# A mixer layer's projections: high and low parts of the activations side by side in one matmul, the two halves summed on VectorE

## The reference

```python
x = x + 0.5 * gate * swiglu(mod(norm(x)), ffn1)        # y (context) the same
hc = mod(norm(y));  pc = hc @ w_in[:, :3072]           # keys fwd, keys bwd, values
s_f, s_b = final states of the two gated recurrences over the context
hx = mod(norm(x));  px = hx @ w_in                     # 8192 columns
o  = bidirectional gated recurrence (8 heads) from px[:, :4096], starting at s_f, s_b
mix = concat(norm(o) * silu(px[:, 4096:5120]), hyena(px[:, 5120:]))
x = x + gate * (mix @ w_out)
x = x + 0.5 * gate * swiglu(mod(norm(x)), ffn2);  return norm(x)
```

## Time and profile before

| | |
|---|---|
| median of 3 runs | 2997.64 us (2997.46 to 2998.92) |
| span of the profiled execution, first to last instruction | 2996.3 us |
| time of the profiled execution beside its span | not recorded |
| TensorE busy | 2959.0 us, 15850 matmuls |
| VectorE busy | 2027.5 us |
| ScalarE busy | 1159.4 us |
| context, HGRN and Hyena stages | 1556.0 to 2152.2 us |

### The profile page before, as it was taken

The page is one execution under the profiler, slowest core; times in us unless marked ns, Lnnn a source line. Parts: engine busy times, 40 slices in busy tenths (PEclk is TensorE's granted clock), DMA queues, the critical chain, the costliest instruction groups (busy, mean ns, idle before and its releaser), DMA issues. The chain is left out here.

```text
span 2996.3 us, 42446 instructions
## 1 busy us (share of the span) xinstructions
PE 2959.0 (99%) x15850; PEld 2521.0 (84%) x15850; DVE 2027.5 (68%) x2558; ACT 1159.4 (39%) x1473; POOL 148.3 (5%) x182
## 2 busy tenths in 40 slices
PE   7999999999999999999999999999999999999998
PEld 3588888888888888888889999999997888888887
DVE  4698667676766677774476567778866666666667
ACT  5322222222122222222247777754445444444444
POOL 3000000000000000000000033340000000000000
PEclk9999999999999999999999999999999999999999
DMA  9865546354566758573335554455565666666664
GB/s 368 333 210 185 180 140 198 128 175 147 161 222 220 253 167 278 187 242 98 97 90 175 174 168 149 150 161 179 166 204 166 187 194 189 189 190 189 192 192 155
DMA packets 369832, 558.00 MB, mean 186 GB/s; under 512 B 17764, under 2 KB 259809, under 8 KB 368946
## 3 DMA queue, kind: packets, MB, share of 16 engines
q1 hardware_dynamic: 364256, 543.05, 57.7%
q0 software_dynamic: 2640, 8.52, 0.9%
q10 hardware_dynamic: 2818, 4.82, 0.4%
HBM read 550.02 MB, written 6.30 MB: 186 GB/s over the span
## 5 line engine op out<-in xcount | busy, mean ns | idle before, releaser
L442 DVE TENSOR_TENSOR w_lo<-raw,w_hi 128x1024 fp32r<-128x1024 f32 x736 | 911.8, 1240 | 696.1 <-ACT w_hi L435 693.9
L435 ACT ACTIVATE w_hi<-raw 128x1024 fp32r<-128x1024 f32 x736 | 777.9, 1059 | 1478.3 <-PE bank L454 1095.0
L711 DVE SCALAR_TENSOR_TENSOR states<-ada_raw,silu_c,states 128x1024 f32<-128x1024 f32 x300 | 375.5, 1281 | 2.3
L452 PE MATMUL bank<-h_hi_early,w_hi 128*128 128x512 f32 x768 | 300.7, 392 | 2.1 <-issue 2.1
L454 PE MATMUL bank<-h_hi_early,w_lo 128*128 128x512 f32 x768 | 298.9, 389 | 0.0
L453 PE MATMUL bank<-h_lo_early,w_hi 128*128 128x512 f32 x768 | 298.8, 389 | 0.0
L458 PE MATMUL bank<-w_hi,h 128*128 128x512 f32 x736 | 287.7, 391 | 1.9 <-DVE h L559 1.3
L460 PE MATMUL bank<-w_lo,h 128*128 128x512 f32 x736 | 286.5, 389 | 0.0
L459 PE MATMUL bank<-w_hi,h 128*128 128x512 f32 x736 | 286.3, 389 | 0.0
L452 PE MATMUL bank<-h_hi_late,w_hi 128*128 128x512 f32 x704 | 274.0, 389 | 0.0
L454 PE MATMUL bank<-h_hi_late,w_lo 128*128 128x512 f32 x704 | 273.9, 389 | 0.0
(11 more groups left out here) (345 smaller groups left out, 4978.7 us busy)
## 6 DMA issues: line engine op xcount, KB each, us to landing
raw<-in_ffn_w_dram SPq DMA_DIRECT2D x528, 512.0 KB, 4.3
ada_raw<-in_ada_w_dram SPq DMA_DIRECT2D x252, 512.0 KB, 4.7
raw<-in_w_in_dram SPq DMA_DIRECT2D x176, 512.0 KB, 3.7
raw<-in_w_out_dram SPq DMA_DIRECT2D x32, 512.0 KB, 4.3
ada_ahead<-in_ada_w_dram SPq DMA_DIRECT2D x20, 512.0 KB, 17.6
raw<-in_ada_w_dram SPq DMA_DIRECT2D x8, 512.0 KB, 18.4
ada_more<-in_ada_w_dram SPq DMA_DIRECT2D x8, 512.0 KB, 6.9
spec<-spec_spill POOLq DMA_DIRECT2D x8, 512.0 KB, 3.9
```

Source lines behind the costliest of these rows:

```text
L435: nc.scalar.activation(w_hi[un.slot(j)][:], raw[un.slot(j)][:], ACT.Copy).then_inc(hi_done, 1)
L442: nc.vector.tensor_tensor(w_lo[un.slot(j)][:], raw[un.slot(j)][:], w_hi[un.slot(j)][:].bitcast(F32), ALU.subtract).then_inc(lo_done, 1)
L452: nc.tensor.matmul(o, w_hi[slot][:, c0:c0 + P], hi, start=start, stop=False, skip_group_check=True)
L711: nc.vector.scalar_tensor_tensor(out=total, in0=src, scalar=silu_c[:, m, t:t + 1], in1=total, op0=ALU.mult, op1=ALU.add).then_inc(done, 1)
```

## The change

The activations' parts become two halves of one tensor (`hc`, `hx`), and so do the weights' (`w_parts`). For a weight block, `paired_unit` has one matmul of 512 moving columns (both halves of the activations times `w_hi`, into a whole bank) and one of 256 (`w_lo` times the high part, onto the first half of the bank). `value_unit` has one of 512 (`w_hi` and `w_lo` side by side move) and one of 256. A part then fills two banks, and parts take banks 0, 1 and 2, 3 in turn. The two halves of a result are summed by VectorE: `join` reduces two banks (1024 numbers a partition) to 512 in SBUF, `join_values` does the same in two instructions, straight to `ctok` or `vtok` in place of ScalarE's copy. ScalarE and the edges read the sum. Joins stand ahead of `rest_unit` in VectorE's step after the part's last unit; the gates, `xq` and `xg` move from j = 3, 7, 11, 19 to j = 4, 8, 12, 20, the context's from 3 (7 for the first pair) and 7 to 4 and 8. TensorE waits for a join before it starts the part after the next. `w_out` and the FFNs keep their matmuls.

```diff
-        w_hi = [sb(f"w_hi{s}", [P, UNIT], F32R) for s in range(RING)]
-        w_lo = [sb(f"w_lo{s}", [P, UNIT], F32R) for s in range(RING)]
+        w_parts = sb("w_parts", [P, 2, RING, UNIT], F32R)
+        w_hi = [w_parts[:, 0, s, :] for s in range(RING)]
+        w_lo = [w_parts[:, 1, s, :] for s in range(RING)]
...
-        hc_hi = sb("hc_hi", [P, KB, CTX], F32R, scope=con)
-        hc_lo = sb("hc_lo", [P, KB, CTX], F32R, scope=con)
+        hc = sb("hc", [P, 2, KB, CTX], F32R, scope=con)
+        hc_hi, hc_lo = hc[:, 0], hc[:, 1]
...
+        x_whole = sb("x_whole", [P, 2, SEQ], scope=hgs)
...
 
-        def value_unit(pe, un, j, kg, o, hi, lo, each=None):
+        def value_unit(pe, un, j, kg, base, hi, lo):
+
+            pe.wait_ge(lo_done, un.number(j) + 1)
+            for k in range(4):
+                kb = 4 * kg + k
+                w0 = k * 256
+                for t in range(TB):
+                    own = slice(t * P, (t + 1) * P)
+                    nc.tensor.matmul(bank[base + t], hi(kb)[:, own], w_parts[:, :, un.slot(j), w0:w0 + 256], start=(kb == 0), stop=False,
+                                     skip_group_check=True)
+                    last = nc.tensor.matmul(bank[base + t][:, 0:256], lo(kb)[:, own], w_hi[un.slot(j)][:, w0:w0 + 256], start=False,
+                                            stop=(kb == KB - 1), skip_group_check=True)
+            last.then_inc(w_used, 1)
+
+        def paired_unit(pe, un, j, kg, base, both, hi, each=None):
 
             pe.wait_ge(lo_done, un.number(j) + 1)
             for k in range(4):
                 kb = 4 * kg + k
                 if each:
                     pe.wait_ge(each, kb + 1)
-                w0 = k * 256
-                for t in range(TB):
-                    own = slice(t * P, (t + 1) * P)
-                    out_t = o[:, t * 256:(t + 1) * 256]
-                    nc.tensor.matmul(out_t, hi(kb)[:, own], w_hi[un.slot(j)][:, w0:w0 + 256], start=(kb == 0 and t == 0), stop=False,
+                for b in range(2):
+                    c0 = k * 256 + b * P
+                    nc.tensor.matmul(bank[base + b], w_hi[un.slot(j)][:, c0:c0 + P], both(kb), start=(kb == 0), stop=False,
                                      skip_group_check=True)
-                    nc.tensor.matmul(out_t, lo(kb)[:, own], w_hi[un.slot(j)][:, w0:w0 + 256], start=False, stop=False,
-                                     skip_group_check=True)
-                    last = nc.tensor.matmul(out_t, hi(kb)[:, own], w_lo[un.slot(j)][:, w0:w0 + 256], start=False, stop=(kb == KB - 1),
-                                            skip_group_check=True)
+                    last = nc.tensor.matmul(bank[base + b][:, 0:256], w_lo[un.slot(j)][:, c0:c0 + P], hi(kb), start=False,
+                                            stop=(kb == KB - 1), skip_group_check=True)
             last.then_inc(w_used, 1)
 
-        def by_head(bank_ap):
-
-            return bank_ap.rearrange("p (a h c) -> p h a c", a=TB, h=2)
+        def join(out, base):
+
+            return nc.vector.reduce_sum(out, banks[:, base:base + 2, :].rearrange("p a (s n) -> p a n s", s=2), mybir.AxisListType.X)
+
+        def join_values(out, base):
+
+            for a in range(TB):
+                ins = nc.vector.reduce_sum(out[:, :, a, :], bank[base + a].rearrange("p (s h c) -> p h c s", s=2, h=2), mybir.AxisListType.X)
+            return ins
 
         def last_sq(kb):
...
+        OUT_BANK = 4
+        CTX_TURN = (4, 7)
+        HG_JOINED, HY_JOINED = 2 * PAIRS, 7 * PAIRS
         MEAN_BANK = (7,) * (PAIRS - 1) + (6,)
...
+        def hg_base(it, part):
+            return 2 * ((5 * it + part) % 2)
+
+        def hy_base(p, c):
+            return 2 * ((3 * p + c) % 2)
 
         def out_unit(k):
...
+                n = 5 * it + j // 4
+                if j % 4 == 0 and n == 0:
+                    pe.wait_ge(joined, 2 * PAIRS)
+                elif j % 4 == 0 and n == 1:
+                    pe.wait_ge(cs["v"], 1 + PAIRS)
+                elif j % 4 == 0:
+                    pe.wait_ge(joined, HG_JOINED + n - 1)
                 if j // 4 == 3:
-                    value_unit(pe, MX, 20 * it + j, j % 4, bank[3][:], lambda k: hx_hi[:, k, :], lambda k: hx_lo[:, k, :])
+                    value_unit(pe, MX, 20 * it + j, j % 4, hg_base(it, 3), lambda k: hx_hi[:, k, :], lambda k: hx_lo[:, k, :])
                 else:
-                    col_unit(pe, MX, 20 * it + j, j % 4, [bank[j // 4][:, 0:256], bank[j // 4][:, 256:512]],
-                             lambda k: hx_hi[:, k, :], lambda k: hx_lo[:, k, :], True)
+                    paired_unit(pe, MX, 20 * it + j, j % 4, hg_base(it, j // 4), lambda k: hx[:, :, k, :], lambda k: hx_hi[:, k, :])
 
             def hg_scores(it, sc):
...
-            def gates(s, d, b, k_ap, g_ap, value):
-
-                ac.wait_ge(w_used, value)
-                nc.scalar.activation(k_ap, bank[b][:], ACT.Sigmoid, scale=-1.0)
-                nc.scalar.activation(g_ap, bank[b][:], ACT.Sigmoid).then_inc(s["gate"], 1)
+            def gates(s, whole, count, k_ap, g_ap):
+
+                ac.wait_ge(joined, count)
+                nc.scalar.activation(k_ap, whole, ACT.Sigmoid, scale=-1.0)
+                nc.scalar.activation(g_ap, whole, ACT.Sigmoid).then_inc(s["gate"], 1)
...
@@ -1919,7 +1956,7 @@
                     for d in range(2):
                         if j == gates_at[d]:
                             ac.wait_ge(cs["kd"], 2 * it)
-                            gates(cs, d, d, flat(ck[:, d]), flat(cg[:, d]), used(un, CTX_END[it][d]))
+                            gates(cs, flat(c_whole[d][:]), 2 * it + d + 1, flat(ck[:, d]), flat(cg[:, d]))
...
 
-                if j in (3, 7):
-                    d = j // 4
-                    gates(xs, d, d, flat(xk[it % 2][:, d]), flat(xa[it % 2][:, d]), used(MX, 20 * it + j))
                 if j in (4, 8):
                     d = j // 4 - 1
+                    gates(xs, flat(x_whole[:]), HG_JOINED + 5 * it + d + 1, flat(xk[it % 2][:, d]), flat(xa[it % 2][:, d]))
                     keys_logs(xs, it, d, flat(xk[it % 2][:, d]), flat(xa[it % 2][:, d]), hg_cols[:, it])
-                if j == 11:
+                if j == 12:
                     if it:
                         ac.wait_ge(xs["kq"], it * 10)
-                    ac.wait_ge(w_used, used(MX, 20 * it + j))
-                    nc.scalar.activation(flat(xq[:]), bank[2][:], ACT.Copy, scale=DK ** -0.5).then_inc(xs["v"], 1)
-                if j == 15:
-                    ac.wait_ge(w_used, used(MX, 20 * it + j))
-                    if it:
-                        ac.wait_ge(xs["ope"], it)
-                    nc.scalar.activation(vtok[:].rearrange("p (h a) c -> p h a c", h=2), by_head(bank[3][:]), ACT.Copy
-                                         ).then_inc(xs["v"], 1)
-                if j == 19:
+                    ac.wait_ge(joined, HG_JOINED + 5 * it + 3)
+                    nc.scalar.activation(flat(xq[:]), flat(x_whole[:]), ACT.Copy, scale=DK ** -0.5).then_inc(xs["v"], 1)
+                if j == 20:
                     if it:
                         ac.wait_ge(xs["mix"], it + 1)
-                    ac.wait_ge(w_used, used(MX, 20 * it + j))
-                    nc.scalar.activation(flat(xg[:]), bank[4][:], ACT.Silu).then_inc(xs["v"], 1)
+                    ac.wait_ge(joined, HG_JOINED + 5 * it + 5)
+                    nc.scalar.activation(flat(xg[:]), flat(x_whole[:]), ACT.Silu).then_inc(xs["v"], 1)
                 if j + 3 in KEY_AT[it][1:]:
                     hg_decays(it, KEY_AT[it].index(j + 3) - 1)
                 if j == READ_AT[it] + 1:
...
                 if j in CONV_AT[p]:
                     c = CONV_AT[p].index(j)
-                    ac.wait_ge(w_used, used(MX, T_HY + 12 * p + 4 * c + 3))
+                    n = 3 * p + c
+                    ac.wait_ge(joined, HY_JOINED + n + 1)
...
-                        ins = nc.scalar.activation(conv[p % 2][:, c, b, :], bank[part_bank(p, c)][:, b * 256:(b + 1) * 256], ACT.Identity,
+                        ins = nc.scalar.activation(conv[p % 2][:, c, b, :], u_whole[n % 2][:, b, :], ACT.Identity,
...
 
+            def ctx_joined(it, d):
+
+                ve.wait_ge(w_used, used(Units(U_CTX, it, 12), CTX_END[it][d]))
+                if it:
+                    ve.wait_ge(cs["gate"], 2 * it + d - 1)
+                join(c_whole[d][:], ctx_base(it, d)).then_inc(joined, 1)
+
+            def ctx_values(it):
+
+                ve.wait_ge(w_used, used(Units(U_CTX, it, 12), 11))
+                if it:
+                    ve.wait_ge(cs["st"], it)
+                join_values(ctok[:, 2].rearrange("p (h a) c -> p h a c", h=2), ctx_base(it, 2)).then_inc(cs["v"], 1)
+
             for it in range(PAIRS):
                 un = Units(U_CTX, it, 12)
                 ve.wait_ge(cs["k"], 2 * it)
```

(37 more changed lines are left out.)

97 lines of the change are left out of this document (50 added, 47 removed).

## The result

The changed kernel takes 3020.39 us (median of 4 runs, 3018.86 to 3022.87) against 2997.66 us before: ratio 1.0076, 95% interval 1.0064 to 1.0088. It is slower, by 22.7 us; the forecast was 14 us slower.

A forecast was written before the change was run, and what follows sets the result against it. TensorE was taken as the bound while VectorE and ScalarE keep ahead. 2996.3 us less 18.4 saved plus 32.5 of stalls gave a 3010.4 us span, a median of 3011.7, say 3012 us; forecast's own range 3004 to 3025, wider range 2985 to 3026.

The forecast's parts named there:

- What bounds the kernel: Whole span: TensorE busy 2959.0 of 2996.3 us; less matmul time shortens the run if ScalarE and VectorE stay ahead.
- The sum: Whole span: 2996.3 less 18.4 saved plus 32.5 us of stalls gives 3010.4, as a median 3011.7 us.
- The saving: Projection matmuls: a weight block takes 346.9 instead of 360.0 ns; 1408 blocks give 18.4 us less.
- The cost of a join: VectorE: 1.24 us per two-bank join, 51 us more work in all, on average hidden in its free time.
- The delay: ScalarE's inputs wait behind VectorE's queued joins: 7.9 us of stalls per whole HGRN period, 32.5 us in all.
- The distance is enough: Rival: the other engines stay far enough ahead; 2979 us, or 2990 with stalls at the tightest places alone; chance 0.22.
- Half the stalls: Rival: fewer table loads or less `xg` delay leave stalls of 13 to 25 us; 2992 to 3004 us; chance 0.17.
- The clock falls: Rival: stalls lower TensorE's clock, up to 13.6 us more, 2 to 4 expected; above 3025 us; chance 0.08.
- The pace doesn't change: Rival: matmul pairs run at three times 120.0 ns, so nothing is gained; 3021 us; chance 0.05.

The follow-up runs named there:

- The run with idle joins: Changed kernel with HGRN joins omitted, ScalarE reading only first halves from PSUM, and same-size VectorE reductions that nobody reads in the joins' places; 3002.39 us, ratio 1.0014.
- Three places: Changed kernel with query join before `w_lo` of t = 31, `xg` at t = 41, part 0's gates and logarithms at t = 45 and 46; 3003.85 us.
- all places: Changed kernel with query join, `xg`, both parts' HGRN gates and logarithms, and joins around the Hyena stage moved; values still joined; 2994.30 us, ratio 0.9987.
- the values apart and the context stage's logarithms moved: All-places kernel with HGRN values as three unjoined 256-column matmuls and the first context pair's logarithms at step 9 instead of 8; 2989.07 us, ratio 0.9971.
- the waits filled: Changed kernel with 512-column matmuls into an unused bank before waits where TensorE idled from t = 39 on; 3019.73 us, ratio 1.0071.

## Why the prediction was right, and where its numbers were off

**What bounds the kernel** was right: time taken from TensorE counts only as long as the other two keep their distance, and they did not.

**The sum.** The span was forecast at 3010.4 us and is 3019.1. Of the 8.7 us between, some 4 are stalls (36.5 us for 32.5), 4 are a saving that came out smaller, and 0.6 lie ahead of the context stage. The median, forecast at 3011.7 us, is off by the same 8.7: the profiled execution takes 1.8 us more than its span and not 1.3, but is itself 0.5 us above the median. So the direction and most of the size came by the mechanism that was forecast; that single waits were placed wrong while their sum came out near is in part luck.

**The saving.** A pair takes (1846.57 - 1844.15) / 7 = 345.7 ns, first and last of eight starts:

```profile
1844.15 0.39 PE L510 MATMUL bank<-hx,w_parts 128*128 128x512 f32 x1
...
1846.57 0.39 PE L510 MATMUL bank<-hx,w_parts 128*128 128x512 f32 x1
```

The forecast was 346.9. But in other units it takes (2007.42 - 2004.94) / 7 = 354.3 ns. Step by step, with 0.105 us a unit taken off, the changed kernel loses 40.4 us against the one before, of which steps with over 0.15 us hold 36.5; the other 3.9 us are spread. The slower pace, which some 100 of the 176 units have, makes an estimated 100 x 8 x (354.3 - 346.9) = 5.9 us, so the term is 12.5 to 14.5 us and not 18.4. The gap of the Trainium skill ("TensorE: Matmul & The Clock Gate", section "Back-to-back issue gap") would make the pair an estimated 325 ns; the trace doesn't agree, with 346 at best.

**The cost of a join** was right (1.21 us for 1.24, values twice 0.68), and so was its total, which lies beside other work in the average. The run with idle joins shows that in its place it isn't free: 2.3 us a head.

**The delay** was the deciding step, and right in kind: places in two queues, not work. Three places gave back 16.5 us and all places 26.1, with the changed kernel's own work; with the values apart and the context stage's logarithms moved it is 31.3. Its size was off, and this is the term that was mis-sized: 75.8 us were forecast for a whole head (70.0 - 2.1 + 7.9), and it takes 77.2. In detail the level 4 keys come 3.15 us late and not 1.3 (the join of the query part at t = 32 was left out), the level 5 keys 6.9 and not 4.6, the level 7 keys 8.1 (1870.70 against 1862.63) and not 6.0. The waits lie elsewhere than forecast: 2.5, 0.9 and 2.95 us at t = 39, 43 and 47 instead of 0.3 at t = 41, 3.1 at t = 43 and 3.5 at t = 47, and none at t = 52. The query join, moved alone, gave 0.3 to 0.6 of the missing 1.4 us; which part of the chain holds the rest was not isolated.

By stage, forecast and measured: context -2.6 and -1.3; t = 0 to 39 +1.6 and +3.1 (136.7 us for 133.7); t = 40 to 79 +11.6 and +14.5; Hyena +3.0 and +5.1; `w_out` +0.5 and +0.6 (its 32 units). The Hyena stage missed most at t = 86 and t = 90, in the tail of the last head.

**The rivals.** *The distance is enough*: no. Even with no join in the HGRN stage the kernel is at 2995.65 us, since the context stage and the last head have no distance either. *Half the stalls*: no. *The clock falls*: it did, five times, which is why the granted clock is 0.996 over the span, but it adds nothing that can be measured (3019.73 us with the waits filled, for 3020.39); the prediction's remark that the lost time is part of the next wait was right, and its 2 to 4 us were too much. *The pace doesn't change*: it did, from 360.0 ns a block to 346 or 354.

## What to carry to other kernels

When a step hands a result to an engine through another engine's queue, ask which instruction stands last before it in that queue and what the receiver has standing behind it; joins of 1.2 us in a queue that is 69% busy made a head 7 us longer here, and moving the same instructions by one or two steps took it back. Where two engines pass work to and fro, the third one's waits are a symptom: shortening one, or keeping the clock up in it, moves it to the next. Change the places first at the one that sets the length of a round, and time rounds, not waits.

## What the runs showed of the hardware that was not expected

- The same pair of matmuls has two paces at the granted clock of 1.00, 346 and 354 ns, constant through a unit of eight pairs but for the first; the kernel before shows nothing of the kind in its matmuls of 256 (70.0 us for each head, to the tenth). What switches between them was not found.
- The length of a wait alone doesn't tell whether the clock falls: in the changed kernel none followed the 3.05 us at t = 27 (the granted clock is 1.00 over that head), while one of 3.4 us followed the 2.51 us at t = 63; with other waits filled, 2.96 us at the same t = 27 was followed by one.
- A join that reads two PSUM banks (1024 elements) takes 1.21 us, one of the same size from SBUF 1.25 us (the idle joins; means of 16 each).
